# A fused layer on one core: one quarter of the expert values gathered by row instead of multiplied

## The chip, the core and the metric

The kernel runs on one core of a Trainium2 chip. The metric is device microseconds of that core; the time before is the median of three runs. The engines are named as the profile names them: PE (matmul), PEld (its weight load, which overlaps PE), DVE, ACT, POOL and SP. SP issues nearly all transfers, from one queue; 16 DMA engines carry them.

## The reference, cut to what matters

One layer with 256 tokens and 2048 channels. First a mixing block (projections, two kinds of linear attention, an output projection, LayerNorm). Then a product-key expert block, which is what the change touches:

```python
experts = ...   # per token 8 heads x 16 picks = 128 expert numbers i*128 + j
gates = softmax(top_s)                                     # per token 128 gates
act = gelu(einsum('tkd,td->tk', u_tab[experts], x))        # 128 activations a token
out = einsum('tk,tkd->td', gates * act, v_tab[experts])    # values, weighted and summed
h = layer_norm(alpha * h + out)
```

Both tables have 128 x 128 rows (experts) of 2048 channels in float32, 128 MB each.

## The kernel before, in words

Nothing is gathered. The kernel reads both tables whole and multiplies densely; the picks enter as a matrix of gates that is zero almost everywhere.

- **U stage, 128 tiles** (tile i holds the 128 experts with that i). SP loads 1 MB of `peer_u` in four pieces (`load_u`), DVE transposes it in quarters (`u_quarter`), ACT rounds it to the high part (`u_high`), POOL subtracts for the low part (`u_low`), PE multiplies (`u_tile`) into one of the PSUM banks 0, 1 and 7. ACT and DVE add the cross term, and ACT applies Gelu (`gelu`). For tiles 0 to 63 (near) the result goes into `act_w[:, 0]`; for tiles 64 to 127 (far) it stays in PSUM until DVE multiplies it into the gates (`weigh`).
- Between tiles 0 and 50 DVE works out the routing beside it (`route_*`): `ijg` gets i, j and gate of each pick. From tile 64 on DVE builds one-hot rows and columns of four tokens (`hot_rows`, `hot_cols`) and PE spreads the gates out by four small matmuls a tile (`spread`), which DVE multiplies into `act_w`. After this `act_w` holds gate times activation of every expert (partition j) for every token.
- **V stage, 128 tiles**, SP's loop over `load_v`: 1 MB of `peer_v` a tile, four slots; tile i is loaded when tile i-4 has been multiplied (`v_free`). ACT makes the high part of the tile's two halves and of the weights (`v_high`: `v_hi`, `m_hi`, `v_hi`), DVE the low parts (`v_low`: L1147 `v_lo`, L1149 `m_lo`, L1151 `v_lo`), and PE multiplies (L1604, `v_products`): high by high, high by low, low by high, for two blocks of 128 tokens (a), two halves of the channels (h) and two banks in each half (c), which is 3 x 2 x 2 x 2 = 24 matmuls of 512 columns a tile. All eight PSUM banks accumulate over all 128 tiles; bank 4a + 2h + c holds 512 channels of 128 tokens. `v_hi` has buffers for two tiles.
- In the V stage SP also loads `n_again`, `ln1g_sb` and `ln1b_sb` behind tile 67, from which POOL rebuilds the layer's input in eight blocks (L1268, L1270, from tile 70 on), and `ln2b_sb` and the last two value tiles (`v_late_raw`) behind tile 99. The last four value tiles are multiplied bank by bank, so that the final LayerNorm of a bank starts while PE is at the next.

The order on each engine is written out by hand; waits are on semaphores. DVE instructions that depend on the one before have a `drain` between them.

Of the kernel before, what the change touches and what calls it, by code (L numbers as in the profile page):

```python
# [25 lines left out]
F32 = mybir.dt.float32  # L26
# [24 lines left out]
U_PICK, U_TURN, U_SPREAD = 25, 51, 64  # L51
UR = 6
# [17 lines left out]
def constants():  # L70
    c = {}
    c["ident"] = np.eye(P, dtype=np.float32)
    c["iota"] = np.broadcast_to(np.arange(P, dtype=np.float32), (P, P))
    half = RDK // 2
    inv = np.float32(10000.0) ** (-np.arange(half, dtype=np.float32) / np.float32(half))
    ang = np.arange(T, dtype=np.float32)[None, :] * inv.astype(np.float32)[:, None]
    c["cos"], c["sin"] = np.cos(ang), np.sin(ang)
    t = np.arange(T)
    c["scan"] = np.broadcast_to((t % CH != 0).astype(np.float32), (P, T))

    m, n = np.meshgrid(np.arange(P), np.arange(P), indexing="ij")
# [7 lines left out]
    c["decay"] = np.concatenate([b for g in LOG_GAMMA for b in tiles(g)], axis=1)  # L89
    pack = lambda names: np.ascontiguousarray(np.concatenate([c[k].astype(np.float32) for k in names], axis=1))  # L90
    return pack(KEEP), pack(MIX)


def build(nc, x, w_in, w_up, b_gate, gla_g, ret_g, w_out, ln1_g, ln1_b, w_q, subkeys, peer_u, peer_v,
          ln2_g, ln2_b, keep_c, mix_c, out):
    ctx = ExitStack()
    with ctx:
# [67 lines left out]
        pick_ig = at("pick_ig", CST + 4608, [P, 2, T])  # L165
# [92 lines left out]
        v_hi_done, m_hi_done, v_lo_done, v_free, sum_done = sem("v_hi_done"), sem("m_hi_done"), sem("v_lo_done"), sem("v_free"), sem("sum_done")  # L258
        last_in, y_done, y_pool, out_done = sem("last_in"), sem("y_done"), sem("y_pool"), sem("out_done")
# [27 lines left out]
        def _(sp):  # L287
# [23 lines left out]
            with nc.allow_non_contiguous_dma(reason="512 bias values, one channel a partition"):  # L311
                sp.dma_start(bias4, b_gate[0].rearrange("(h p) -> p h", p=P)).then_inc(wup_in, 16)
            load(1, win, GQ + COL)
# [55 lines left out]
            with sp.Fori(U_TWO // 2, P // 2) as ii:  # L369
                for s in range(2):  # L370

                    sp.wait_ge(ut_done, ii * 8 + 4 * s - 4)
                    load_u(ii * 2 + s, s)

# [5 lines left out]
            for s in range(2):  # L380
                sp.wait_ge(ut_done, 4 * (P - 1) + 4 * s)
                load_v(s, s)
            sp.wait_ge(uparts_free, UR + 4 * P)
            for s in range(2, 4):
                load_v(s, s)

# [15 lines left out]
            for s in range(2):  # L402
                sp.dma_start(v_late_raw[:, 2 * s:2 * s + 2, :].rearrange("p a b -> p (a b)"), v_rows[P - 2 + s].rearrange("j d -> j d")).then_inc(v_late, 16)
            with sp.Fori(P // 4 - 7, P // 4 - 1) as ii:
                for s in range(4):
                    sp.wait_ge(v_free, ii * 8 + 2 * s + 2)
                    load_v(ii * 4 + s, s)
            for s in range(2):
                sp.wait_ge(v_free, (P // 4 - 1) * 8 + 2 * s + 2)
                load_v(P - 4 + s, s)  # L410
# [31 lines left out]
        def _(act):  # L442
# [42 lines left out]
            act.dma_start(keepc[:], keep_c).then_inc(keep_in, 16)  # L485
# [100 lines left out]
            def gelu(ii, j, far):  # L586

                act.wait_ge(u_sum, ii * 6 + j + 1)
                z = u_bank(j)[:, 0:T]
                act.activation(z if far else tile_w(0, ii * 6 + j), z if far else by_four(z), ACT.Gelu).then_inc(gelu_done, 1)  # L590
# [29 lines left out]
            for i in range(U_TURN // 6 * 6, U_SPREAD + 2):  # L620
                u_tile(i // 6, i % 6, 1)
                if i == U_TURN + 1:
                    act.wait_ge(ijg_mm, 1)
                    act.activation(pick_ig[:], ps[:, 4:6, 0:T], ACT.Copy).then_inc(ijg_sb, 1)
                elif U_TURN + 1 < i < U_TURN + 10:
                    ones(2 * (i - U_TURN - 2))
                    ones(2 * (i - U_TURN - 2) + 1)
            with act.Fori(U_SPREAD // 6 + 1, P // 6) as ii:
                for j in range(6):
                    u_tile(ii, j, 1, far=True)  # L630
# [89 lines left out]
        def _(dve):  # L720
# [345 lines left out]
            route_pick(1, 1, 2, 1)  # L1066
            with dve.Fori(U_TURN // 6, U_SPREAD // 6) as ii:
# [32 lines left out]
            def weigh(ii, j):  # L1100

                i = ii * 6 + j
                dve.drain()
                dve.wait_ge(gelu_done, i + 1)
                w = tile_w(1, i - P // 2)
                dve.tensor_tensor(w, w, by_four(u_bank(j)[:, 0:T]), ALU.mult).then_inc(gelu_free, 1)
# [21 lines left out]
            with dve.Fori(U_UNROLL // 6, P // 6) as ii:  # L1128
                for j in range(6):
                    u_spread_tile(ii, j)  # L1130
# [9 lines left out]
            def v_low(ii, s, half, last=False):  # L1140
# [6 lines left out]
                dve.tensor_tensor(lo_v[:, n, :], raw_v[:, n, :], vh[0].bitcast(F32), ALU.subtract)  # L1147
                dve.wait_ge(m_hi_done, ii * 4 + s + 1)
# [9 lines left out]
            with dve.Fori(1, P // 8) as ii:  # L1158
                for s in range(4):
                    v_low(ii, s, 0)  # L1160
            with dve.Fori(P // 8, P // 4 - 1) as ii:
# [7 lines left out]
            def last_bank(a, b):  # L1169

                c = slice(b * COL, (b + 1) * COL)
                dve.wait_ge(sum_done, 4 * a + b + 1)
                dve.scalar_tensor_tensor(h1_again[:, a, c], h1_again[:, a, c], float(ALPHA), bank(4 * a + b), ALU.mult, ALU.add).then_inc(bank_read, 1)
# [21 lines left out]
            dve.memset(power[:], -0.5)  # L1195
            for b in range(4):
                last_bank(0, b)
# [7 lines left out]
            last_bank(1, 3)  # L1205
# [6 lines left out]
        def _(pool):  # L1212
# [50 lines left out]
            pool.wait_ge(n_in, 48)  # L1263
            for a in range(TT):
                for b in range(4):
                    o, n_in_order = part(h1_again[:, a, :], 4 * b, 4), n_again[:, a, :].rearrange("p (f q l) -> p q f l", f=KT, q=4)[:, :, 4 * b:4 * b + 4, :]
                    pool.wait_ge(v_free, VRING + 2 * (P // 2 + 6 + 4 * a + b))
                    pool.tensor_tensor(o, n_in_order, part(ln1g_sb[:], 4 * b, 4), ALU.mult)  # L1268
                    pool.drain()
                    pool.tensor_tensor(o, o, part(ln1b_sb[:], 4 * b, 4), ALU.add).then_inc(h1_ready, 1)  # L1270
# [16 lines left out]
        def _(pe):  # L1287
# [308 lines left out]
            def v_products(s, h, a, start=False, last=False, stop=False, cs=range(2)):  # L1596
# [5 lines left out]
                for p, (m, v) in enumerate(((mh, vh), (mh, vl), (ml, vh))):  # L1602
                    for c in cs:
# [30 lines left out]
            for a in range(TT):  # L1634
                for b in range(4):
# [27 lines left out]
```

## Time and profile before

| | |
|---|---|
| time, median of 3 runs | 2042.71 us (2042.55 to 2043.31) |
| span of the profiled execution, first to last instruction | 2047.0 us |
| first and last start of a value matmul (L1604) | 1339.1 and 2035.5 us |
| PE busy | 2029.4 us, 99% |
| DVE busy | 1229.1 us, 60% |
| POOL busy | 1115.0 us, 54% |
| bytes moved | 381.35 MB |

No other time is given for the profiled execution than its span; it is 4.3 us (0.2%) above the median of the unprofiled runs. A busy time is the sum of an engine's instruction times. PE's instructions overlap, so its busy share tells only that it is never idle: the time of a matmul in a row of them is read from the chain, a stretch of time divided by the count.

### The profile page before, as it was taken

What the parts mean: (1) busy time and instruction counts of PE and PEld (TensorE: products, weight loads), DVE (VectorE), ACT (ScalarE), POOL (GpSimd) and SP (SyncE); (2) the same over time, 40 slices, a digit from 0 to 9 for tenths busy, and PEclk for the clock granted to TensorE, in tenths of its full rate; (3) what the DMA queues carried; (4) which work ended last, traced back from release to release, by engine and by line L of the source; (5) the groups of instructions that cost most, each with busy time, mean ns of one, the idle gap of its engine ahead of it and who ended that gap; (6) DMA issues with size and microseconds to landing.
All of it is one profiled execution on the core that took longest, in us unless ns stands there. A gap on an engine that the chain in (4) does not pass through costs nothing.

```text
span 2047.0 us, 34143 instructions
## 1 busy us (share of the span) xinstructions
PE 2029.4 (99%) x11214; PEld 1764.3 (86%) x11214; DVE 1229.1 (60%) x2134; ACT 980.1 (48%) x1454; POOL 1115.0 (54%) x720
## 2 busy tenths in 40 slices
PE   9999999999999999999999999999999999999997
PEld 8998888889988888888888888888888888888886
DVE  1753121122888777558998988955555556655556
ACT  4544334445455565674444444444444444444443
POOL 6877778877788989888777777700000002200001
PEclk9999999999999999999999999999999999999999
DMA  8555656577688887776666666665555557556552
GB/s 291 169 152 170 193 172 215 177 205 196 155 182 192 191 186 173 176 187 166 162 160 161 162 162 164 164 226 185 198 192 190 200 187 278 191 191 260 187 198 86
DMA packets 153540, 381.35 MB, mean 186 GB/s; under 512 B 19808, under 2 KB 22496, under 8 KB 135680
## 3 DMA queue, kind: packets, MB, share of 16 engines
q1 hardware_dynamic: 153328, 380.32, 64.9%
q8 instruction: 42, 0.69, 0.1%
q14 instruction: 26, 0.21, 0.0%
q10 hardware_dynamic: 144, 0.13, 0.0%
HBM read 376.20 MB, written 4.19 MB: 186 GB/s over the span
## 4 chain that ended last, share of the span: by engine, by line
PE 91%; POOL 3%; issue 3%; DVE 1%; DMA 1%; ACT 0%; DVEq 0%; POOLq 0%; ACTq 0%; SPq 0%
PE ps L1604 33%; PE ps L1563 22%; PE ps L1564 11%; PE ps L1303 7%; PE ps L1304 7%; PE ps L1305 7%; PE ps L1545 3%; POOL w_lo L1217 2%; POOL u_lo L1255 1%; PE ps L1419 1%; DMA raw<-in_w_in 0%; PE ps L1299 0%; PE ps L1528 0%; PE ps L1437 0%; DMA v_raw<-in_peer_v 0%
## 5 line engine op out<-in xcount | busy, mean ns | idle before, releaser
L1563 PE MATMUL ps<-xT,u_hi 128*128 128x512 f32 x2048 | 727.5, 399 | 0.5 <-POOL u_lo L1255 0.5
L1255 POOL TENSOR_TENSOR u_lo<-u_t,u_hi 128x512 fp32r<-128x512 f32 x512 | 653.1, 1298 | 129.4 <-ACT u_hi L579 127.2
L1564 PE MATMUL ps<-xT,u_lo 128*128 128x256 f32 x2048 | 573.3, 280 | 0.0
L579 ACT ACTIVATE u_hi<-u_t 128x512 fp32r<-128x512 f32 x512 | 321.2, 632 | 360.1 <-DVE u_t L961 359.5
L1217 POOL TENSOR_TENSOR w_lo<-raw,w_hi 128x1024 fp32r<-128x1024 f32 x174 | 424.1, 2449 | 107.5 <-ACT w_hi L448 101.2
L1563 PEld LDWEIGHTS ps<-xT,u_hi 128*128 128x128 f32 x2048 | 384.7, 188 | 90.7 <-issue 0.6
L961 DVE STREAM_TRANSPOSE u_t<-u_raw 128x512 f32<-128x512 f32 x512 | 356.0, 702 | 105.8 <-PE ps L1564 72.8
L1564 PEld LDWEIGHTS ps<-xT,u_lo 128*128 128x128 f32 x2048 | 386.6, 189 | 0.0
L1604 PE MATMUL ps<-v_hi,m_hi 128*128 128x512 f32 x1024 | 317.9, 389 | 0.0
L1604 PE MATMUL ps<-v_hi,m_lo 128*128 128x512 f32 x1024 | 317.8, 389 | 0.0
L448 ACT ACTIVATE w_hi<-raw 128x1024 fp32r<-128x1024 f32 x175 | 184.8, 1059 | 271.7 <-PE ps L1305 265.2
L1604 PE MATMUL ps<-v_lo,m_hi 128*128 128x512 f32 x1008 | 311.6, 389 | 0.0
L1268 POOL TENSOR_TENSOR h_again<-n_again,ln1g_sb 128x512 f32<-128x512 f32 x8 | 10.3, 1292 | 406.4 <-PE ps L1604 406.4
L1147 DVE TENSOR_TENSOR v_lo<-v_raw,v_hi 128x1024 fp32r<-128x1024 f32 x126 | 154.4, 1225 | 128.7 <-ACT v_hi L658 128.7
L1604 PEld LDWEIGHTS ps<-v_hi,m_hi 128*128 128x128 f32 x1024 | 192.1, 188 | 40.3 <-DVE m_lo L1149 0.5
L1604 PEld LDWEIGHTS ps<-v_hi,m_lo 128*128 128x128 f32 x1024 | 192.2, 188 | 40.0
L1604 PEld LDWEIGHTS ps<-v_lo,m_hi 128*128 128x128 f32 x1008 | 189.2, 188 | 39.3
L658 ACT ACTIVATE v_hi<-v_raw 128x1024 fp32r<-128x1024 f32 x124 | 131.6, 1061 | 159.2 <-PE ps L1604 146.6
L1151 DVE TENSOR_TENSOR v_lo<-v_raw,v_hi 128x1024 fp32r<-128x1024 f32 x126 | 163.0, 1293 | 45.2 <-ACT v_hi L663 45.2
L1303 PE MATMUL ps<-xT,w_hi 128*128 128x256 f32 x640 | 183.7, 287 | 3.5 <-DVE xT L716 3.1
L1305 PE MATMUL ps<-xT,w_lo 128*128 128x256 f32 x640 | 181.6, 284 | 0.0
L1304 PE MATMUL ps<-xT,w_hi 128*128 128x256 f32 x640 | 181.6, 284 | 0.0
(206 smaller groups left out, 2341.4 us busy)
## 6 DMA issues: line engine op xcount, KB each, us to landing
u_raw<-in_peer_u SPq DMA_DIRECT2D x512, 256.0 KB, 4.8
v_raw<-in_peer_v SPq DMA_DIRECT2D x126, 1024.0 KB, 4.9
raw<-in_w_in SPq DMA_DIRECT2D x111, 512.0 KB, 3.8
raw<-in_w_out SPq DMA_DIRECT2D x32, 512.0 KB, 4.8
raw<-in_w_peer_q SPq DMA_DIRECT2D x128, 128.0 KB, 3.4
x_again<-in_x SPq DMA_DIRECT2D x1, 2048.0 KB, 8.2
n_dram<-n_perm SPq DMA_DIRECT2D x1, 2048.0 KB, 8.1
n_again<-n_dram SPq DMA_DIRECT2D x1, 2048.0 KB, 9.3
```

The source lines that it names most:

```text
L448: act.activation(w_hi[:, k % HI_RING, :], raw[:, k, :], ACT.Copy).then_inc(hi_done, 1)
L579: act.activation(u_hi[:, slot(j, f), :], u_t[:, slot(j, f), :], ACT.Copy).then_inc(uhi_done, 1)
L961: dve.transpose(u_t[:, slot(j, f), :].rearrange("p (f b l) -> p b f l", f=4, b=4), u_raw[s][:].rearrange("p (b f l) -> p b f l", b=4, l=32 ...
L1151: dve.tensor_tensor(lo_v[:, n + 1, :], raw_v[:, n + 1, :], vh[1].bitcast(F32), ALU.subtract).then_inc(v_lo_done, 1)
L1217: pool.tensor_tensor(w_lo[:, k, :], raw[:, k, :], w_hi[:, k % HI_RING, :].bitcast(F32), ALU.subtract).then_inc(lo_done, 1)
L1255: pool.tensor_tensor(u_lo[:, r, :], u_t[:, r, :], u_hi[:, r, :].bitcast(F32), ALU.subtract).then_inc(ulo_done, 1)
L1303: pe.matmul(o, lh, rh, start=start, stop=False, skip_group_check=lint)
L1304: pe.matmul(o, lh, rl, start=False, stop=False, skip_group_check=lint)
L1305: return pe.matmul(o, ll, rh, start=False, stop=stop, skip_group_check=lint)
L1563: pe.matmul(acc, u_hi[:, r, c], xT[:, :, kt, :], start=kt == 0, stop=False)
L1564: ins = pe.matmul(acc[:, 0:T], u_lo[:, r, c], xT_hi[:, kt, :], start=False, stop=kt == KT - 1)
L1604: ins = pe.matmul(bank(4 * a + 2 * h + c), m, v[:, c * 512:(c + 1) * 512], start=start and p == 0, stop=stop and p == 2)
```

## The change

Bank 7 (tokens 128 to 255, channels 1536 to 2047) is no longer accumulated by PE. For each of these 128 tokens and each of its 128 picks, the quarter row of `peer_v` (512 channels, 2 KB) is gathered by POOL with an indirect DMA, one pick of all 128 tokens at a time, and DVE adds it, times gate and activation, into bank 7. For this:

- DVE works out two addresses a pick behind the routing (`place_picks`, tile 48). ACT writes them and the gates to DRAM.
- The activations are written to DRAM before the gates are multiplied in: the near ones in four transfers of 1 MB issued by ACT from tile 66 on, the far ones tile by tile by SP (64 KB each), for which ACT applies Gelu a second time to the upper 128 tokens (`far_act`). The Gelu of a far tile now goes into the other half of its bank.
- The gates for the one-hot columns are read from PSUM (bank 5) and no longer from SBUF.
- At the start of the V stage POOL loads addresses and gates, then issues 128 indirect DMAs that fetch one activation a token each (4 bytes x 128), then 128 that fetch rows, into eight slots. A row slot is refilled when DVE has added it. The eight blocks of L1268 and L1270 stand between the row groups 6 to 13.
- DVE waits for all activations at tile 44, multiplies them by the gates, and adds two rows in each of the tiles 44 to 107, between L1147 and L1149.
- PE's matmuls for (a, h) = (1, 1) take c = 0 alone: 21 a tile. In the last four tiles seven banks are left of eight.
- `v_late_raw` moves to where the row slots were, and its two transfers move behind the load of tile 123, after a wait for the last row. `h1_again` moves. Bank 7 is read first at the end, no longer last.

The diff, cut:

```diff
+            def far_store(n, s):
+                sp.wait_ge(far_done, n + 1)
+                sp.dma_start(act_far[bass.ds(n, 1)].rearrange("i j t -> (i j) t"), far_act[:, s, :]).then_inc(far_out[s], 16)
...
-            for s in range(2):
-                sp.dma_start(v_late_raw[:, 2 * s:2 * s + 2, :]..., v_rows[P - 2 + s]...).then_inc(v_late, 16)
             with sp.Fori(P // 4 - 7, P // 4 - 1) as ii:
                 for s in range(4):
                     sp.wait_ge(v_free, ii * 8 + 2 * s + 2)
                     load_v(ii * 4 + s, s)
+            sp.wait_ge(row_added, P)
+            for s in range(2):
+                sp.dma_start(v_late_raw[:, 2 * s:2 * s + 2, :]..., v_rows[P - 2 + s]...).then_inc(v_late, 16)
...
+                    act.activation(far_act[:, j % 2, :], z[:, P:T], ACT.Gelu).then_inc(far_done, 1)
+                act.activation(u_bank(j)[:, T:2 * T] if far else tile_w(0, ii * 6 + j), z if far else by_four(z), ACT.Gelu).then_inc(gelu_done, 1)
...
-                    ins = dve.tensor_scalar(hot_i[:, k, :], iota_ps, pick_ig[:, 0, t], pick_ig[:, 1, t], ALU.is_equal, ALU.mult)
+                    ins = dve.tensor_scalar(hot_i[:, k, :], iota_ps, pick_i[:, t], bank(5)[:, t], ALU.is_equal, ALU.mult)
...
+            def row_add(n, c):
+                dve.drain()
+                dve.wait_ge(row_in[c], n * 16 + 16)
+                dve.scalar_tensor_tensor(bank(7), sp_rows[:, c, :], sp_w[:, bass.ds(n * S_CHUNK + c, 1)], bank(7), ALU.mult, ALU.add).then_inc(row_added, 1)
...
+            dve.wait_ge(picks_in, 32)
+            dve.wait_ge(act_in, 16 * P)
+            dve.tensor_tensor(sp_w[:], sp_w[:], sp_gate[:], ALU.mult)
...
+            pool.wait_ge(uparts_free, UR + 4 * P)
+            for k in range(P):
+                pool.indirect_dma_start(sp_w[:, k:k + 1], None, act_dram, bass.IndirectOffsetOnAxis(ap=sp_at[:, 0, k:k + 1], axis=0)).then_inc(act_in, 16)
+            for n in range(S_END):
+                row_gather(n)
+                if n > 5 and n < 14:
+                    h1_block((n - 6) // 4, (n - 6) % 4)
...
-                    for c in cs:
+                    for c in cs if (a, h) != (1, 1) else (0,):
```

## Rows read from the trace of the kernel before

**Rows 1.** The page: span, then busy time and instructions of engines.
```profile
span 2047.0 us, 34143 instructions
PE 2029.4 (99%) x11214; PEld 1764.3 (86%) x11214; DVE 1229.1 (60%) x2134; ACT 980.1 (48%) x1454; POOL 1115.0 (54%) x720
```
**Rows 2.** The chain that ended last, in order of time: start, us, what.
```profile
1339.23 663.72 PE ps L1604 x2928
2002.97 4.99 DMA v_raw<-in_peer_v
...
2015.91 20.03 PE ps L1604 x87
```
**Rows 3.** Windows: busy us (instructions) of each engine, PEclk, DMA share, GB/s.
```profile
1180.00:1339.00 159.00, 159.00 (x983) 141.68 (x982) 142.24 (x291) 76.56 (x148) 121.52 (x95) 1.00 0.65 160
1360.00:1579.00 219.00, 219.00 (x968) 181.35 (x967) 115.69 (x121) 97.38 (x121) 0.00 (x0) 1.00 0.56 192
1690.00:1700.00 10.00, 10.00 (x46) 8.29 (x45) 4.88 (x7) 4.86 (x6) 0.00 (x0) 1.00 1.02 428
```
**Rows 4.** Waits from 1345 to 2000 us: us in total, times, longest.
```profile
ACT m_hi L661 <- PE ps L1604: 207.2, 118, 1.8
ACT v_hi L658 <- PE ps L1604: 145.4, 117, 1.4
DVE v_lo L1147 <- ACT v_hi L658: 126.9, 112, 5.0
...
ACT v_hi L658 <- DMA v_raw<-in_peer_v: 11.3, 4, 5.1
```
**Rows 5.** Timeline near the end: three DVE instructions with no wait between them.
```profile
2005.63 1.22 DVE L1147 TENSOR_TENSOR v_lo<-v_raw,v_hi 128x1024 fp32r<-128x1024 f32 x1
...
2006.77 0.42 DVE L1149 TENSOR_TENSOR m_lo<-act_w,m_hi 128x256 fp32r<-128x256 f32 x1
...
2007.10 1.22 DVE L1151 TENSOR_TENSOR v_lo<-v_raw,v_hi 128x1024 fp32r<-128x1024 f32 x1
```
**Rows 6.** Groups by form on DVE: count, busy us, mean ns, idle before.
```profile
L1090 DVE TENSOR_SCALAR hot_i<-ps,pick_ig 128x128 f32<-128x128 f32 x256 | 84.9, 394 | 0.0
...
L1098 DVE TENSOR_TENSOR act_w<-act_w,ps 128x512 f32 x54 | 37.1, 688 | 12.1 <-issue 12.1
...
L1173 DVE SCALAR_TENSOR_TENSOR h_again<-h_again,ps 128x512 f32<-128x512 f32 x8 | 5.5, 682 | 5.0 <-PE ps L1604 5.0
...
L704 DVE SCALAR_TENSOR_TENSOR h_again<-h_again,small,ps 128x512 f32<-128x512 f32 x5 | 3.7, 739 | 0.0
```
**Rows 7.** DMA issues on SP: count, KB each, median us from issue to landing.
```profile
u_raw<-in_peer_u SPq DMA_DIRECT2D x512, 256.0 KB, 4.8
v_raw<-in_peer_v SPq DMA_DIRECT2D x126, 1024.0 KB, 4.9
...
v_late_raw<-in_peer_v SPq DMA_DIRECT2D x2, 1024.0 KB, 10.3
...
ln1b_sb<-in_ln_b SPq DMA_DIRECT2D x1, 1024.0 KB, 13.3
```
**Rows 8.** POOL's groups, all forms: count, busy us, mean ns.
```profile
L1255 POOL TENSOR_TENSOR u_lo<-u_t,u_hi 128x512 fp32r<-128x512 f32 x512 | 653.1, 1298 | 129.4 <-ACT u_hi L579 127.2
...
L1217 POOL TENSOR_TENSOR w_lo<-raw,w_hi 128x1024 fp32r<-128x1024 f32 x174 | 424.1, 2449 | 107.5 <-ACT w_hi L448 101.2 <-DVE n_perm L927 6.2
```
**Rows 9.** Line L378, the issue of a value load: min/median/max ns.
```profile
L378 SPq DMA_DIRECT2D v_raw<-in_peer_v x126: 328/333/433, 1324.3 to 2003.0; - x126
```
**Rows 10.** Timeline where POOL's first block runs beside DVE.
```profile
1720.21 1.29 POOL L1268 TENSOR_TENSOR h_again<-n_again,ln1g_sb 128x512 f32<-128x512 f32 x1 [387.49 <-PE ps L1604]
...
1720.79 1.00 DVE L1149 TENSOR_TENSOR m_lo<-act_w,m_hi 128x256 fp32r<-128x256 f32 x1 [1.09 <-ACT m_hi L661]
1721.64 1.28 POOL L1270 TENSOR_TENSOR h_again<-h_again,ln1b_sb 128x512 f32<-128x512 f32 x1
1721.71 2.31 DVE L1151 TENSOR_TENSOR v_lo<-v_raw,v_hi 128x1024 fp32r<-128x1024 f32 x1
```

More of the change, by code:

```diff
@@ L51 @@
 U_PICK, U_TURN, U_SPREAD = 25, 51, 64
+FAR_COL = D - COL
+S_CHUNK, S_FIRST = 8, 11
+S_END = -(-P // S_CHUNK)
 UR = 6
@@ L385, in _ @@
                 load_v(s, s)
+            for s in range(2):
+                far_store(P // 2 - 2 + s, s)
             sp.wait_ge(spread_mm, P - U_SPREAD)
@@ L589, in gelu @@
                 z = u_bank(j)[:, 0:T]
-                act.activation(z if far else tile_w(0, ii * 6 + j), z if far else by_four(z), ACT.Gelu).then_inc(gelu_done, 1)
+                if far:
+                    if not isinstance(ii, int) or ii * 6 + j >= P // 2 + 2:
+                        act.wait_ge(far_out[j % 2], 16 * (ii * 3 + j // 2 - P // 4))
+                    act.activation(far_act[:, j % 2, :], z[:, P:T], ACT.Gelu).then_inc(far_done, 1)
+                act.activation(u_bank(j)[:, T:2 * T] if far else tile_w(0, ii * 6 + j), z if far else by_four(z), ACT.Gelu).then_inc(gelu_done, 1)
             def u_tile(ii, j, late=0, far=False):
@@ L623, in _ @@
                     act.wait_ge(ijg_mm, 1)
-                    act.activation(pick_ig[:], ps[:, 4:6, 0:T], ACT.Copy).then_inc(ijg_sb, 1)
+                    act.activation(pick_i[:], bank(4)[:, 0:T], ACT.Copy).then_inc(ijg_sb, 1)
+                    act.wait_ge(picks_done, 1)
+                    act.dma_start(at_dram, pick_at[:].rearrange("p s k -> p (s k)")).then_inc(picks_out, 16)
+                    act.dma_start(gate_dram, ijg[:, 2, 1, :]).then_inc(picks_out, 16)
                 elif U_TURN + 1 < i < U_TURN + 10:
+                    if i == U_TURN + 2:
+                        act.wait_ge(picks_out, 32)
                     ones(2 * (i - U_TURN - 2))
                     ones(2 * (i - U_TURN - 2) + 1)
-            with act.Fori(U_SPREAD // 6 + 1, P // 6) as ii:
+            for j in range(6):
+                u_tile(U_SPREAD // 6 + 1, j, 1, far=True)
+                if j < 4:
+                    if j == 0:
+                        act.wait_ge(gelu_done, P // 2)
+                    act.dma_start(act_near[:, 2 * K * j:2 * K * (j + 1)],
+                                  act_w[:, 0, P // 4 + 8 * j:P // 4 + 8 * (j + 1)].rearrange("p q i t -> p (q i t)")).then_inc(near_out, 16)
+            with act.Fori(U_SPREAD // 6 + 2, P // 6) as ii:
                 for j in range(6):
@@ L1066, in _, with place_picks @@
             route_pick(1, 1, 2, 1)
+            def place_picks():
+                i, j = ijg[:, 0, 1, :], ijg[:, 1, 1, :]
+                near, far, later, row = (pick_tmp[:, n, :] for n in range(4))
+                dve.wait_ge(tok_in, 16)
+                dve.drain()
+                dve.tensor_scalar(near, j, float(P * P // 2), tok[:, 1:2], ALU.mult, ALU.add)
+                dve.tensor_scalar(far, i, float(P * P), tok[:, 0:1], ALU.mult, ALU.add)
+                dve.tensor_scalar(later, i, float(P // 2), None, ALU.is_ge)
+                dve.tensor_scalar(row, j, float(D // COL), float(D // COL - 1), ALU.mult, ALU.add)
+                dve.drain()
+                dve.scalar_tensor_tensor(near, i, 4.0, near, ALU.mult, ALU.add)
+                dve.scalar_tensor_tensor(far, j, float(P), far, ALU.mult, ALU.add)
+                dve.scalar_tensor_tensor(pick_at[:, 1, :], i, float(P * D // COL), row, ALU.mult, ALU.add)
+                dve.drain()
+                dve.tensor_tensor(far, far, near, ALU.subtract)
+                dve.drain()
+                dve.tensor_tensor(far, far, later, ALU.mult)
+                dve.drain()
+                dve.tensor_tensor(pick_at[:, 0, :], far, near, ALU.add).then_inc(picks_done, 1)
+            place_picks()
             with dve.Fori(U_TURN // 6, U_SPREAD // 6) as ii:
@@ L1127, in _ @@
                 u_spread_tile(i // 6, i % 6, spreads=i > U_SPREAD + 1, weighs=i > U_SPREAD + 2)
-            with dve.Fori(U_UNROLL // 6, P // 6) as ii:
+            with dve.Fori(U_UNROLL // 6, 16) as ii:
+                for j in range(6):
+                    u_spread_tile(ii, j)
+            dve.wait_ge(near_out, 64)
+            with dve.Fori(16, P // 6) as ii:
                 for j in range(6):
@@ L1261, in _, with h1_block @@
                 u_low(P // 6, n)
[L1263 to L1270, printed above, removed]
+            def h1_block(a, b):
+                o, n_in_order = part(h1_again[:, a, :], 4 * b, 4), n_again[:, a, :].rearrange("p (f q l) -> p q f l", f=KT, q=4)[:, :, 4 * b:4 * b + 4, :]
+                pool.wait_ge(n_in, 48)
+                pool.wait_ge(v_free, VRING + 2 * (P // 2 + 6 + 4 * a + b))
+                pool.tensor_tensor(o, n_in_order, part(ln1g_sb[:], 4 * b, 4), ALU.mult)
+                pool.drain()
+                pool.tensor_tensor(o, o, part(ln1b_sb[:], 4 * b, 4), ALU.add).then_inc(h1_ready, 1)
@@ L1634, in _ @@
             for a in range(TT):
-                for b in range(4):
+                for b in range(4 - a):
                     for s in range(4):
```

89 lines of the change are left out of this document (74 added, 15 removed).

## The prediction

> **What bounds the kernel now.** I read the page first: PE is busy for 99% of the span [rows 1], so any gain must take work from PE. The chain that ended last gives the place: the value stage begins at 1339.2 us, and from there the chain is PE alone for 663.72 us and 2928 matmuls, and after a short passage through one transfer, ACT and DVE for another 20.03 us and 87 matmuls [rows 2]. That is 226.7 ns a matmul and, with 24 in a tile, 5.44 us a tile. The windows show that in this stage PE is never idle, at the full clock (2.4 GHz), DVE is busy 115.7 of 219 us, POOL not at all, and the DMA engines 0.56 of the time at 192 GB/s [rows 3]. The waits say who follows whom: ACT waits for PE to free the halves, DVE for ACT, and transfers are waited for 11.3 us in all [rows 4]. So in this stage PE is the bound and DVE, POOL and the transfers have room. In the last stretch of the U stage the picture is tighter: DVE 142 of 159 us, still with PE never idle [rows 3].
>
> **The change, part by part.**
>
> PE loses three matmuls in each of 128 tiles: 384 x 226.7 ns = -87.1 us [rows 2], if nothing else becomes the bound. A tile then takes 21 x 0.2267 = 4.76 us.
>
> DVE. Back to back, the three instructions of a tile start 1.14 and 0.33 us apart, and the third I count at 1.14 again: 2.61 us a tile [rows 5]. Before, that hides under 5.44. A row's addition is a scalar_tensor_tensor over 512 elements with one operand in PSUM and a scalar from SBUF; L704 is that form at 0.74 us, L1173 with a constant takes 0.68 [rows 6]. Writing to PSUM, not SBUF, I count at nothing. The drain in front costs what L1098 shows in a loop, 12.1 us over 54 = 0.22 us [rows 6]. A row is then 0.96 us, two of them 1.92, and a tile 2.61 + 1.92 = 4.53 us against PE's 4.76. So PE stays the bound in tiles 44 to 107 with 0.23 us to spare; I take 0 for this, and its bound above is 64 tiles times what DVE is over (0.3 us more a row would make 5.13 us a tile: +24 us). The U stage's DVE share of 0.89 without an idle PE [rows 3] says that an engine this full need not cost PE anything.
>
> POOL. No row shows an indirect DMA. The nearest prices are SP's issue of a load, 0.33 us [rows 9], below, and a POOL instruction over 1024 elements, 2.45 us [rows 8], above. I take the 512-element one, 1.30 us. The far activation of the last tile leaves ACT about 1 us into the V stage, its store stands behind two value loads (1 MB lands in 4.9 us [rows 7]) and the addresses are loaded after it, so the gathers start some 11 us in. 128 activation gathers end at 11 + 128 x 1.30 = 177 us, and DVE needs them at tile 44, at some 43 x 4.76 = 205 us. So there is no stall up to 1.5 us a gather. Row gathers need two a tile, 2.6 of 4.76 us, and eight slots are four tiles of lead, 19 us. I take 0; at 2.45 us the activations end at 325 us, 120 us late.
> The Trainium skill gives the price that no row here has: first byte of a transfer issued by POOL about 1 us ("DMA: Bandwidth & Descriptors", Latency and other measured facts), which as an estimate would end the activations 139 us into the stage, also hidden. The same page's fixed cost of about 2.0 us a transfer (Anatomy of one DMA) would, if POOL were held for all of it, end them at 267 us and stall DVE by some 60; the page calls it mostly completion, which POOL need not await.
>
> Transfers. A tile moves 1.05 MB, now in 4.76 us, plus 0.52 MB of rows: 330 GB/s in tiles 44 to 107. A window with a backlog shows 428 GB/s at share 1.02 [rows 3], so 330 fits, at about 0.8. The load of a tile is issued 4 tiles ahead, and ACT takes it up about 1.57 tiles later, 7.5 us against 4.9 to land. Behind tile 67 come 4 MB of other loads (the last of them landing after 13.3 us [rows 7]). Before, four waits of 11.3 us on ACT came out of it and the like, none on PE [rows 3, 4]. With shorter tiles and rows in between, 5 MB + 1.5 MB at about 400 GB/s land some 18 us after tile 63 is done, and PE needs them prepared by 19.0 - 4.3 = 14.8 us: +4 us, once.
>
> POOL's eight blocks. Beside one of them m_lo takes 1.00 and v_lo 2.31 us [rows 10] against 0.42 and 1.22 [rows 5]: 1.67 us more of DVE a block. Before, this lay in DVE's idle time. Now a block comes every fourth tile or so, and four tiles have 0.9 us of slack plus about 2 us by which DVE is ahead of PE. I count 0.75 us a block, +6 us.
>
> The U stage. `place_picks` is ten small instructions with drains, some 4 us of DVE once, under the ring of six quarters by which DVE is ahead. The one-hot columns now read a scalar from PSUM: each of four a tile takes 0.39 us [rows 6]; a scalar costs 0.06 (L704 against L1173), so up to that again, 0.24 us a tile, lies in DVE's 0.7 us of free time a tile. ACT's second Gelu is 128 elements beside 48% busy [rows 3]. The four near stores put 1 MB each beside a u tile of 1 MB that lands in 4.8 us; a tile here takes 6.6 us, so some lateness is taken up by the ring. SP's store waits for a Gelu that comes a tile before SP's next load is due. Together +3 us, between 0 and 64 x 0.2 = 13.
>
> The end. The late loads now stand behind tile 123: 3 MB are in the queue when tile 124 is loaded, and 2 MB took 10.3 us [rows 7]. Tile 125 lands as long after its issue as before (4.99 us [rows 2]) but two tiles of PE are now 1.4 us shorter: +1 us. DVE's last banks are reached with one application in front of bank 6: +1 us.
>
> Sum: -87.1 + 4 + 6 + 3 + 2 = -72 us on the span of 2047.0, which is 0.2% over the median; taken from the median, 2042.7 - 72 = 1971 us.
>
> **The rivals.**
>
> *DVE or the transfers become the bound of tiles 44 to 107.* For it: 0.23 us of slack is small, and the shares of the windows give another reading of the transfers: loads of the V stage at 192/0.56 = 343 GB/s, of the U stage, cut into shorter runs as the gathered rows are, at 160/0.65 = 246 [rows 3]; then a tile needs 3.06 + 2.13 = 5.19 us, +28 us. Against it: 428 GB/s in one window. With DVE 0.3 us over a row it is +24. Either gives about 1997, both together no more than 2010.
>
> *POOL is late.* At 2.0 us a gather the activations end at 267 us, +62: 2033. Beyond 2.08 us the change is slower than before, and at 2.45 it gives 1971 + 120 = 2091 us. For it: nothing but the missing row.
>
> *The gathers hold DVE off, the case on the other side.* 2.57 us of POOL work cost DVE 1.67 us in rows 10, 0.65 us for each. If address reading and issuing did the same, the 166 us of activation gathers would leave DVE 35% of its rate, 7.5 us a tile: 22 tiles in place of 35, +62 us; and two gathers a tile would add 1.69 to 4.53, 6.2 us a tile, 64 x 1.46 = +93. Together 1971 + 155 = 2126. It decides from 0.3 us lost for each us on, where it costs the 72.
> The Trainium skill says that a DVE instruction with two SBUF inputs contends with a POOL instruction that reads SBUF, one blocking the other wholly ("SBUF — State Buffer", Who interferes with whom); rows 10 agree (1.00 and 2.31 us). The page infers that descriptor generation needs only the write side, which `tensor_tensor` leaves free; taken so, this rival costs nothing, and taken as a POOL instruction like any other it costs the 155.
>
> *The change moves nothing*: not to be had, since the 384 matmuls are gone; it could only be hit by two costs that cancel.
>
> **How the numbers follow.** The forecast, PE the bound with small costs, 0.52; its own range 1956 (the 87.1 alone) to 1990. DVE or transfers the bound, 1990 to 2010: 0.18. POOL between 1.5 and 2.08 us a gather, or a mix of these, 2010 to 2038: 0.12. POOL beyond that or holding DVE off, above 2047: 0.16. The rest, 0.02, within 0.2% (4 us), which is about what a measurement of this kernel can tell from no change. Faster 0.82, same 0.02, slower 0.16. The range of 8 in 10 is 1956 to 2028: it leaves out the slower cases and the top of the third.
>
> **What would show it.** Right: 21 matmuls a tile at 227 ns in the value stage, PE never idle, a value stage of 610 to 625 us; POOL's gathers at 1.5 us or less; DVE at some 0.95 of the window in tiles 44 to 107, its rows at 0.74 us, v_lo still 1.22 us. Wrong: PE waiting for m_lo in every tile (DVE or rows late); a long wait of DVE at tile 44 for an activation; v_lo and m_lo longer throughout; ACT waiting for `v_raw`; PE idle in the U stage.

## The result and the profile after

The changed kernel takes 2022.9 us (median of 4 runs, 2014.9 to 2028.0) against 2043.0 (2042.6 to 2043.6): ratio 0.990, 95% interval 0.9873 to 0.9927. That is 20 us faster where 72 were forecast. The profiled execution, the slowest of the four, took 2028.0 us, with a span of 2026.2, 20.8 below that of [rows 1]. The page's first lines, and its two groups of indirect DMAs:

```profile
span 2026.2 us, 34413 instructions
PE 1962.4 (97%) x10830; PEld 1701.2 (84%) x10830; DVE 1311.5 (65%) x2274; ACT 989.1 (49%) x1518; POOL 1438.3 (71%) x978
...
L1392 POOL DMA_INDIRECT sp_rows<-in_peer_v,sp_at x128 | 160.1, 1251 | 76.7 <-DVE ps L1231 49.6
...
L1404 POOL DMA_INDIRECT sp_w<-act_dram,sp_at x128 | 158.7, 1240 | 48.3 <-issue 48.3
```

The 384 matmuls are gone, and PE now has idle time that [rows 1] did not have. The chain shows where (start, us, what; it answers to [rows 2]):

```profile
1339.24 209.68 PE ps L1742 x924
1548.92 14.23 issue
1563.16 8.06 PE ps L1742 x21
1571.29 7.73 another core or an unknown queue
1580.18 93.62 PE ps L1742 x399
1673.96 18.97 DMA v_raw<-in_peer_v
...
1697.72 21.52 PE ps L1742 x84
1719.25 8.14 issue
1727.38 15.24 PE ps L1742 x54
...
1870.56 107.80 PE ps L1742 x462
```

The stage starts at 1339.2 as before. Its first 44 tiles (924 matmuls) take 209.68 us: 226.9 ns a matmul, 4.77 us a tile. Then PE stops at 1548.9, 1575.5, 1687.9 and 1719.2 us, and for 3.6 us at 1867. Of the 21 matmuls at 1563.16 the first 14 start 439 ns apart, the rest 227 ns again: the granted clock is at half (1.2 GHz) until 1569.3. The waits from 1330 to 2020 us (in total, times, longest), beside [rows 4], name what was late:

```profile
ACT v_hi L718 <- DMA v_raw<-in_peer_v: 69.1, 32, 13.0
POOL sp_rows L1392 <- DVE ps L1231: 49.6, 39, 7.1
POOL sp_w L1404 <- issue: 48.3, 128, 6.1
...
POOL h_again L1382 <- issue: 43.4, 8, 8.4
...
PEld ps L1742 <- DVE m_lo L1244: 26.8, 12, 10.1
...
DVE ps L1231 <- DMA sp_rows<-in_peer_v,sp_at: 18.4, 9, 8.6
DVE sp_w L1259 <- DMA sp_w<-act_dram,sp_at: 16.1, 1, 16.1
POOL sp_at L1398 <- DMA act_dram<-far_act: 15.6, 1, 15.6
```

The windows (columns as in [rows 3]) show that the loss sits in a few places and is not a rate of every tile:

```profile
1360.00:1540.00 180.00, 180.00 (x796) 149.05 (x795) 108.89 (x113) 91.42 (x115) 142.62 (x112) 1.00 0.66 221
1540.00:1600.00 60.00, 41.43 (x157) 33.04 (x156) 30.06 (x37) 17.66 (x22) 36.40 (x35) 0.80 0.67 212
1600.00:1660.00 60.00, 60.00 (x266) 49.69 (x265) 51.43 (x63) 30.13 (x38) 33.67 (x26) 1.00 0.92 326
1660.00:1700.00 40.00, 30.34 (x129) 24.72 (x128) 25.86 (x31) 15.48 (x20) 13.43 (x11) 0.90 0.95 374
1700.00:1740.00 40.00, 31.86 (x124) 25.64 (x123) 24.88 (x30) 13.22 (x16) 19.35 (x16) 0.84 0.55 189
```

From 1600 to 1660, with two rows in every tile, PE is never idle and the clock is 1.00. From 1540 to 1600, 1660 to 1700 and 1700 to 1740 it is idle for 18.6, 9.7 and 8.1 us, and the granted clock is 0.80, 0.90 and 0.84: each of these pauses is followed by matmuls at 1.2 GHz.

The starts of L1742's matmuls give the ledger. The last one begins at 2013.1, so the stage takes 674 us where 128 tiles of 4.76 would be 609. Of the 65 us over it, tiles 43 to 46 have 25, tiles 67 and 68 have 12, tiles 71 and 72 have 11, tiles 88 to 100 have 8.5 (6.4 of it in tiles 99 and 100), the last four tiles 6.4 (two gaps of 2 us and the slow matmuls behind them), and the rest, 1.5, is small.

### The profile page after: what moved, and what is told of

The parts are those of the page before. It is cut to its first block, busy times and chain, and to the rows that moved or that the text cites. A ratio compares the mean times of both kernels' runs of the same rounds, so it can differ in the third digit from the quotient of the medians.

```text
span 2026.2 us, 34413 instructions
## 1 busy us (share of the span) xinstructions
PE 1962.4 (97%) x10830; PEld 1701.2 (84%) x10830; DVE 1311.5 (65%) x2274; ACT 989.1 (49%) x1518; POOL 1438.3 (71%) x978
## 4 chain that ended last, share of the span: by engine, by line
PE 78%; issue 7%; POOL 6%; DMA 3%; DVE 3%; DVEq 1%; ACT 1%; another core or an unknown queue 0%; POOLq 0%; SPq 0%; ACTq 0%
PE ps L1742 23%; PE ps L1701 20%; PE ps L1702 10%; PE ps L1441 7%; PE ps L1443 7%; PE ps L1442 7%; PE ps L1683 3%; POOL w_lo L1329 2%; POOL u_lo L1367 2%; DMA v_raw<-in_peer_v 1%; DMA sp_rows<-in_peer_v,sp_at 1%; DVEq L1229 1%; DVE v_lo L1240 1%; DMA u_raw<-in_peer_u 1%; DVE ps L1231 1%
## 5 line engine op out<-in xcount | busy, mean ns | idle before, releaser
L1742 PE MATMUL ps<-v_hi,m_hi 128*128 128x512 f32 x896 | 297.2, 400 | 44.7 <-issue 22.4
L1742 PE MATMUL ps<-v_hi,m_lo 128*128 128x512 f32 x896 | 293.3, 395 | 0.0
L1742 PE MATMUL ps<-v_lo,m_hi 128*128 128x512 f32 x882 | 287.9, 395 | 0.0
L1742 PEld LDWEIGHTS ps<-v_hi,m_hi 128*128 128x128 f32 x896 | 171.2, 193 | 85.9 <-DVE m_lo L1244 26.8
L1240 DVE TENSOR_TENSOR v_lo<-v_raw,v_hi 128x1024 fp32r<-128x1024 f32 x126 | 157.1, 1247 | 90.3 <-ACT v_hi L718 86.2
L1392 POOL DMA_INDIRECT sp_rows<-in_peer_v,sp_at x128 | 160.1, 1251 | 76.7 <-DVE ps L1231 49.6
L1742 PEld LDWEIGHTS ps<-v_hi,m_lo 128*128 128x128 f32 x896 | 171.7, 192 | 36.6
L1742 PEld LDWEIGHTS ps<-v_lo,m_hi 128*128 128x128 f32 x882 | 169.2, 192 | 36.1
L1404 POOL DMA_INDIRECT sp_w<-act_dram,sp_at x128 | 158.7, 1240 | 48.3 <-issue 48.3
```

The costliest lines, as they stand in the source:

```text
L1742: ins = pe.matmul(bank(4 * a + 2 * h + c), m, v[:, c * 512:(c + 1) * 512], start=start and p == 0, stop=stop and p == 2)
```

## The experiments

All times are medians, all ratios to the kernel before as run on the same chip. The unchanged kernel's own median there was 2042.8, 2044.0 and 2045.2 us in the three sittings.

**Rows begin one step later (e1_first12).** DVE takes up the rows at tile 48, not 44.
```
-S_CHUNK, S_FIRST = 8, 11
+S_CHUNK, S_FIRST = 8, 12
```


> The first row addition is moved from tile 44 to tile 48, nothing else. Theory A (the wait for the last activation at tile 44, and PE's lower clock behind it, cost the 25 us by which tiles 43 to 46 are longer than 4.76 us): the activations end at 1558 us, tile 48 is reached by DVE at about 1561, so the stall goes and the time falls by 20 to 25 us, to about 2000. Rival B (tiles with additions are as slow as DVE, POOL or the transfers make them, and the stall only comes out of that): the time stays within 8 us of the changed kernel, at 2015 to 2028. In both the long tiles 67, 68, 71 and 72 stay, or the last two get shorter, since the row groups come four tiles later beside POOL's blocks.

1993.3 us, ratio 0.9755 [0.9737, 0.9773]: 30 us less than the change as it stands. The wait of DVE for an activation is 2.7 us in place of 16.1, and in the stretch that had 18.6 us of idle PE and a clock of 0.80:
```profile
1540.00:1600.00 60.00, 58.86 (x259) 48.05 (x258) 44.36 (x54) 29.57 (x37) 42.80 (x35) 1.00 0.86 308
```
The 30 us are more than the 20 to 25 expected, because the move did two things. By tile, in the profiled executions, tiles 43 to 46 lose their excess of 25 us (1.5 comes back in tiles 47 and 50). Tiles 71 and 72 lose theirs of 11 as well, now that the rows come four tiles later beside POOL's blocks, and tiles 67 and 68 grow by 2. The late activations, about 24 us, are still the largest single loss.

**POOL's blocks behind all row gathers (e2_blocks_last).**
```
 for n in range(S_END):
     row_gather(n)
-    if n > 5 and n < 14:
-        h1_block((n - 6) // 4, (n - 6) % 4)
+for n in range(8):
+    h1_block(n // 4, n % 4)
```


> POOL's eight blocks (two instructions with a drain between) stand behind the last row gather, no longer between the row groups. Theory A (the drain of POOL waits 5.4 us on the mean for gathers still under way, 43.4 us in all, and the rows behind it come late): the gaps before the second instruction of a block go, the tiles 71, 72, 88, 89, 96, 99 and 100 lose their excess of 20 us together, and the time falls by 12 to 20 us. Rival B (those tiles are long because DVE's low parts are held by POOL's two instructions, as in the kernel before): the gaps go too, but the additions still take their time and the time falls by less than 6 us. The stall at tile 44 stays in both.

2013.4 us, 0.9847 [0.9831, 0.9864]: -9.5, between the two expectations (12 to 20, under 6) and not much beside the 13 us over which the change's own four runs spread. The pause at tile 71 is gone, the one behind tile 67 stays, and some of the gain goes back in tiles 106 to 108 (7.3, 6.5 and 5.3 us), where the eight blocks now run back to back beside DVE. Of their drains only the first, right behind the last gathers, leaves a gap: 5.8 us, against 0.14 in the other seven.

**The same, with the 4 MB of other loads spread (e3_blocks_last_loads_spread).** Eight pieces of 0.5 MB, one behind every third tile's load from tile 69 on.
```
+for i in range(P // 2 + 4, P - 28):
+    sp.wait_ge(v_free, 2 * i + 2)
+    load_v(i, i % 4)
+    if i % 3 == 0 and once:
+        sp.dma_start(*once.pop(0)).then_inc(n_in, 16)
```


> As the kernel with the blocks last, and the 4 MB that SP loads behind tile 67 (layer input, gain, bias) are cut into eight pieces of 0.5 MB, one behind every third tile from 69 on. Theory A (this burst keeps the value loads behind it waiting, 12 us in tiles 67 and 68): another 10 to 12 us less than with the blocks last alone, and ACT's longest wait for a value load falls from 13.0 to under 4 us. Rival B (the transfers are at their limit throughout the tiles with rows, so the 4 MB cost the same wherever they stand): less than 4 us, the waits are spread over more tiles.

1997.2 us, 0.9784 [0.9760, 0.9808]: -16 against e2. The same stretch in e2 and then here:
```profile
1660.00:1700.00 40.00, 29.07 (x129) 23.78 (x128) 24.34 (x31) 15.48 (x20) 15.30 (x13) 0.90 0.97 378
```
```profile
1660.00:1700.00 40.00, 39.42 (x174) 32.32 (x174) 33.30 (x41) 19.64 (x26) 21.25 (x17) 1.00 0.96 346
```
The DMA engines were at 0.97 and 0.96. What PE gained is 174 matmuls for 129, because the value loads no longer stand behind a burst: from 1640 to 1700 ACT's longest wait for `v_raw` is 13.8 us in e2 and 3.4 here.

**All three together (e5_all_moved).** Besides, the two late loads are issued inside the last tile loads.
```
+if i in (P - 12, P - 9):
+    s = (i - P + 12) // 3
+    sp.wait_ge(row_added, P)
+    sp.dma_start(v_late_raw[:, 2 * s:2 * s + 2, :]..., v_rows[P - 2 + s]...)
```


> All moved: first addition at tile 48, blocks last, the 4 MB spread, and the two loads of the last value tiles put behind the loads of tiles 116 and 119 in place of behind tile 123. Theory A (four separate waits, none of them a rate): PE without a pause and at its full clock from tile 0 to 123, 4.76 us a tile, the time at 2042.7 - 87 + 6 = 1962 us, between 1957 and 1972. Rival B (a rate of DVE, POOL or the transfers of about 5 us in tiles with rows): 16 us more, 1975 to 1990.

1976.4 us, 0.9663 [0.9644, 0.9682]: 4 us above the 1957 to 1972 of theory A and inside the 1975 to 1990 of rival B, so the time alone speaks for B. The windows speak against it. Two windows, in the stage's middle and where the blocks now run:
```profile
1580.00:1700.00 120.00, 119.98 (x529) 99.00 (x529) 104.56 (x127) 60.67 (x76) 66.58 (x50) 1.00 0.94 341
```
```profile
1840.00:1880.00 40.00, 35.06 (x152) 27.80 (x151) 35.58 (x35) 18.38 (x23) 25.71 (x18) 1.00 0.73 247
```
With rows in each tile and 341 GB/s, PE is idle for 0.02 of 120 us: neither DVE's 4.5 us a tile (the forecast's sum) nor the transfers are a bound. What is left is 8 us in tiles 107 to 112 (109 and 110 take 7.3 each), where the blocks run back to back, 3.8 in tiles 99 and 100, where SP loads `ln2b_sb` whole, and 4.2 in tiles 47 and 48.

**No gathers and no additions (f1_no_gather).** This leaves the gathered rows out of the result, and the waits on them with it.
```
-for k in range(P):
-    pool.indirect_dma_start(sp_w[:, k:k + 1], ...)
 for n in range(S_END):
-    row_gather(n)
```


> The changed kernel without its 256 gathers and 128 additions (and the waits on them): bank 7 of the values is left out of the output. All stores of the U stage stay. Theory A (the 384 matmuls are worth 87 us, and the U stage's additions cost nothing): 2042.7 - 87 + 2 to 5 = 1958 to 1961 us, ACT and DVE with less work than before. The burst behind tile 67 costs a few us at most, since no rows compete with it. Rival B (the 21-matmul tile is itself limited by ACT, DVE or loads): over 1970 us.

1966.7 us, 0.9619 [0.9603, 0.9635]. The stage's last matmul starts at 1953.7, 614.7 us after its first. So 77 of the 87 us are there once the gathers and additions are gone. The time lies between the two expectations (1958 to 1961, over 1970). Of the missing 10 us, 5 are in the stage, which is 614.7 us where 128 tiles would be 609: 1.4 in tile 67 (the burst) and 3.6 in the last four tiles (the late loads), both still in place here. One more is behind the last matmul, 12.4 us against 11.4; the rest this run does not place.

**A semaphore in place of the drain in a block (s1_sem_for_drain).**
```
-pool.tensor_tensor(o, n_in_order, part(ln1g_sb[:], 4 * b, 4), ALU.mult)
-pool.drain()
+pool.tensor_tensor(o, n_in_order, part(ln1g_sb[:], 4 * b, 4), ALU.mult).then_inc(h1_half, 1)
+pool.wait_ge(h1_half, 4 * a + b + 1)
```


> The changed kernel with the drain between POOL's two instructions of a block replaced by a semaphore that the first one raises and the second waits for; the blocks stay between the row groups. Theory A (the drain waits for gathers that POOL has issued and that are still in work; the first instruction itself is done after 1.3 us): the gap before the second instruction falls from 5.4 us to under 0.3 us, rows are no longer late behind a block, and the time falls by 8 to 15 us. Rival B (the first instruction's writes, or POOL itself, are held up for those 5 us by something else, such as DVE's reads): the gap stays at about 5 us and so does the time.

2014.5 us, 0.9856 [0.9839, 0.9872]: -8.5; its four runs (2012.7 to 2015.7) just overlap the change's (2014.9 to 2028.0), so the rows say more than the time. The first block on POOL's timeline after the change, with the gathers behind it, and then here:
```profile
1709.88 1.32 POOL L1380 TENSOR_TENSOR h_again<-n_again,ln1g_sb 128x512 f32<-128x512 f32 x1 [26.52 <-PE ps L1742]
1717.18 1.29 POOL L1382 TENSOR_TENSOR h_again<-h_again,ln1b_sb 128x512 f32<-128x512 f32 x1 [5.97 <-issue]
1718.61 0.98 POOL L1392 DMA_INDIRECT sp_rows<-in_peer_v,sp_at  x1
```
```profile
1707.83 1.32 POOL L1381 TENSOR_TENSOR h_again<-n_again,ln1g_sb 128x512 f32<-128x512 f32 x1 [25.78 <-PE ps L1743]
1709.23 1.29 POOL L1383 TENSOR_TENSOR h_again<-h_again,ln1b_sb 128x512 f32<-128x512 f32 x1
1710.66 0.99 POOL L1393 DMA_INDIRECT sp_rows<-in_peer_v,sp_at  x1
```
The 6 us between the halves of a block were the drain, waiting for gathers in flight, as the single long one of e2 says too; over eight blocks 43.4 us, here 0.6. Tile 71 falls from 13.1 to 8.3 us, yet PE still pauses for 3.8 while gathers go out unbroken. That asked for the next group.

**The low part of the values by a one-input instruction (g3_one_input).** The low part is then the value itself and the result differs; the instruction's price on DVE is that of the two-input form (1.22 us in both).
```
-dve.tensor_tensor(lo_v[:, n, :], raw_v[:, n, :], vh[0].bitcast(F32), ALU.subtract)
+dve.tensor_reduce(lo_v[:, n, :], raw_v[:, n, :].unsqueeze(2), AX.X, ALU.add)
```


> The changed kernel with DVE's two v_lo instructions of a tile made from one SBUF input in place of two (a reduction over one element, as many elements out; the low part is then the value itself, so the output differs). Theory A (a gather is held from 0.94 to about 1.95 us where DVE is in an instruction with two SBUF inputs; its long ones end as v_lo does): the gathers of activations take 0.94 to 1.1 us each, 1.25 to 1.35 from start to start, the last ends 160 to 175 us after the first in place of 201, and DVE does not wait at tile 44. Rival B (the long gathers come from the loads that share the transfer engines, or from the gather's own bookkeeping): a mean of 1.24 us and 201 us as before, DVE's wait of 16 us stays.

2157.6 us (2 runs), 1.0554 [1.0533, 1.0575]: 135 us slower than the change, which neither theory had. The gathers did get shorter, but this alone does not clear the two-input form, since DVE hardly ran beside them (15 instructions in the window below):
```profile
L1406 POOL DMA_INDIRECT sp_w<-act_dram,sp_at x128 | 121.3, 947 | 47.6 <-issue 47.6
```
But while they go out, PE hardly does (window, then PE's timeline):
```profile
1360.00:1545.00 185.00, 44.75 (x125) 29.16 (x124) 13.18 (x15) 10.95 (x14) 126.25 (x134) 0.57 0.14 40
```
```profile
1417.40 0.59 PE L1744 MATMUL ps<-v_lo,m_hi 128*128 128x512 f32 x1 [2.21 <-issue]
1420.20 0.59 PE L1744 MATMUL ps<-v_hi,m_lo 128*128 128x512 f32 x1 [2.21 <-issue]
```
PE waits for nothing here that the profile shows; its matmuls come 2.8 us apart. So it goes in the second half of tiles 7, 8 and 9, with one matmul in 0.7 to 3.5 us, and in front of each of these tiles PE stands still for 26 to 31 us. So two explanations were tried next: the new DVE form, or the unbroken train of gathers.

**One input without gathers (r1_one_input_no_gather), and one input with paced gathers (p1_one_input_paced).** The pace holds activation gather k until PE has passed tile k/3.
```
+    pool.wait_ge(v_free, VRING + 2 * (k // 3 + 1))
     pool.indirect_dma_start(sp_w[:, k:k + 1], None, act_dram, ...)
```


> The kernel with one-input low parts and no gathers and no additions at all (bank 7 and the low parts differ). Theory A (the gathers slow PE, not the DVE form): 4.76 us a tile throughout and within 3 us of the kernel without gathers, 1966.7 us. Rival B (the DVE form does): long tiles 6 to 9 again and over 2080 us.

> The kernel with one-input low parts (its output differs) and the activation gathers paced: gather k waits until PE has multiplied tile k/3, so about three a tile, 1.59 us apart on the mean in place of 1.25. Theory A (an unbroken train of gathers 1.25 us apart slows the other engines' sequencers, which is why PE's matmuls stood 2.8 us apart in tiles 6 to 9 of the kernel with one-input low parts): tiles 6 to 9 take 4.76 us each, and the time falls from 2157 by at least 120 us. A short slow patch at the first tiles is possible, where the pace lets twelve through at once. Rival B (the other form of DVE instruction slows PE, or the loads): tiles 6 to 9 stay long, about 2150 us.

1966.8 us, 0.9616 [0.9593, 0.9640], and 2012.7 us, 0.9841 [0.9820, 0.9862]. The window of g3 in r1, then in p1:
```profile
1360.00:1545.00 185.00, 185.00 (x818) 153.19 (x817) 111.22 (x117) 94.47 (x117) 0.00 (x0) 1.00 0.64 221
```
```profile
1360.00:1545.00 185.00, 180.83 (x781) 147.80 (x780) 105.60 (x111) 88.68 (x111) 109.91 (x118) 0.98 0.63 211
```
The DVE form does not slow PE. A pace on the same gathers gives back 145 us, and what is left of the slow stretch are tiles 6 and 7 (11.1 and 6.8 us), where the gathers let through by the first waits go out unbroken. What it is in the unbroken train that stops the other engines, no run shows.

**The kernel before once more (p0_before_again)**, unchanged, one profiled run.

> The kernel before, once more, for a second profile. Its first profile has a span of 2047.0 us, 4 us over the median time, while every changed kernel's span is 1.8 us under the time of the same execution. Theory A (that first profiled execution was a slow one by some 6 us, ahead of the value stage): this span is about 2041 us and the value stage begins at 1333 us, so that the changed kernels, which begin it at 1336 to 1339, carry 3 to 6 us from the U stage. Rival B (the first profile was an ordinary one): 2047 us and 1339 us again, and the U stage costs nothing.

2046.2 us, span 2044.4, value stage from 1336.7 to 2033.0: between the two expectations. The start of the stage moves by 2 to 4 us from run to run in both kernels (1336.7 and 1339.1 before, 1335.9 to 1340.3 in the changed ones), so the U stage's part of the change costs nothing that shows beyond that.

**The best of these (b1_spaced), and with the pace (b2_spaced_paced).** e5, with one block a tile from tile 111 on and ln2b loaded in four pieces.
```
-pool.wait_ge(v_free, VRING + 2 * (P // 2 + 6 + 4 * a + b))
+pool.wait_ge(v_free, VRING + 2 * (P - 16 + 4 * a + b))
```


> The kernel with everything moved, and two more steps: POOL's eight blocks wait for tiles 111 to 118, one a tile, and the load of the last bias (1 MB behind tile 99) is cut into four pieces. Theory A (back to back, the blocks hold DVE to a third of its rate over tiles 107 to 112, 9 us in all, and the 1 MB behind tile 99 costs the 4 us of tiles 99 and 100): both excesses go, 10 to 13 us less than with everything moved, 1963 to 1967 us. Rival B (tiles 99 and 107 to 112 are long because the value loads are late from transfers at 0.95 of their capacity all along): 1972 to 1978 us, with ACT's waits for loads of some 97 us unchanged and the long tiles elsewhere.

> The kernel with everything moved and spaced (1967.4 us), and the activation gathers paced by PE's tiles as well (k/3). Theory A (what is left at tile 47, 1.6 us, is the end of an unbroken train): tile 47 back at 4.76 us, the time lower by 1 to 3 us, hardly to be told from none. Rival B (pacing lets the gathers end later than the additions need them): tile 47 longer than 6.4 us and a time over 1969 us.

1967.4 us, 0.9625 [0.9602, 0.9647], and 1965.8 us, 0.9610 [0.9594, 0.9626]: 77 and 79 us under the kernel before in the same sitting and some 56 under the change, as fast as the kernel that gathers nothing. In f1 the late loads and the burst were still in place, so this equality does not make the gathers free: b1's stage is 615.3 us, 6 more than 128 tiles of 4.76. With every gather and every addition in it, b2's middle looks so:
```profile
1560.00:1860.00 300.00, 295.22 (x1298) 242.97 (x1298) 256.13 (x311) 147.56 (x185) 164.89 (x127) 1.00 0.95 344
```
The pace makes no difference that can be measured here (the intervals overlap). Tile 47, which theory A had back at 4.76 us, stays at 6.4, and tile 49 takes 7.8. That the two-input form breaks the train by itself, so that a pace has nothing to add, is our reading.

## Why the prediction was right and wrong

The forecast was 1971 us, with a range of its own from 1956 to 1990; 2022.9 lies outside that, and inside the wide range of 8 in 10 (1956 to 2028). It also lies in the band of 2010 to 2038 that the forecast gave to gathers of 1.5 to 2.08 us or a mixture, at 0.12. The price did come out in there, at 1.57. But by the forecast's own sum this price would have added 7 us and not 52, so that the band was hit by several terms together. Two of its signs of being wrong were seen, the long wait of DVE at tile 44 and ACT waiting for `v_raw`.

**Right: the 87.1 us.** 21 matmuls a tile at 227 ns, and PE never idle where nothing is late (1360 to 1540, 1600 to 1660). f1 keeps 77 of it, b2 79.

**Right: DVE stays under PE, and the transfers fit.** A row's addition takes 0.756 us and a wait of 0.2 in front, 0.96 in all, as forecast; tiles stay at 4.76. DVE's share from 1600 to 1660 is 0.86 and not 0.95, since the two waits of 0.2 us a tile don't count as busy. The forecast 330 GB/s were 326 to 344, though at a share of 0.92 to 0.95, not 0.8. The DVE-or-transfers rival is out: at 5.19 us a tile 120 us would hold 485 matmuls, and e5 has 529.

**Right: the gathers do not hold DVE off.** While the activation gathers go out, L1240's v_lo takes 1225 to 1227 ns, L1246's 1211 to 1248 and m_lo 424 to 427, against 1.22 and 0.42 in [rows 5], so the slower case (2126 us) is out. The longer ones (v_lo up to 2.32 us) come later, beside POOL's blocks. It is the other way round. The timeline of all engines:
```profile
1380.25 0.94 POOL L1404 DMA_INDIRECT sp_w<-act_dram,sp_at  x1 [0.30 <-issue]
...
1381.41 1.23 DVE L1240 TENSOR_TENSOR v_lo<-v_raw,v_hi 128x1024 fp32r<-128x1024 f32 x1 [1.09 <-ACT v_hi L718]
...
1381.50 1.95 POOL L1404 DMA_INDIRECT sp_w<-act_dram,sp_at  x1 [0.30 <-issue]
...
1383.76 0.94 POOL L1404 DMA_INDIRECT sp_w<-act_dram,sp_at  x1 [0.31 <-issue]
1383.86 1.22 DVE L1246 TENSOR_TENSOR v_lo<-v_raw,v_hi 128x1024 fp32r<-128x1024 f32 x1 [0.41 <-ACT v_hi L723]
```
A gather takes 0.94 us, also when v_lo begins behind it, but 1.95 when it starts early in a v_lo that is running. Of the 128 activation gathers 39 start with more than 0.15 us of a v_lo left, and 37 of these take over 1.2 us; no other one takes over 1.03. A row gather that starts inside a row addition (39 do) is not held either: 0.94 to 0.98. That it takes the two-input form of v_lo shows from p1 beside b2, with the same pace: 16 gathers of p1 start in this way in the one-input v_lo and take 0.94 to 1.03, 44 of b2 in the two-input one and take 1.12 to 1.97, 1.96 in the middle. The Trainium skill ("SBUF — State Buffer", Who interferes with whom) infers that descriptor generation is left free by `tensor_tensor`. By that, DVE is indeed not delayed, but POOL is, so the inference holds for one side only.

**Wrong: "POOL, 0 us" (1.30 us a gather from 11 us in, done at 177).** The step that failed is the price taken for a gather and the date of the first. The price was good for one gather (1.25 from start to start), but the mean over the train, with three in ten held by DVE, was 1.57: 200 us from the first start to the last where 166 were forecast. And the first gather starts at 1355.8, 16.6 us in and not 11, since the address load waits for the far store (15.6 us) and then has to land. The last starts at 1555.8, which is 217 us in, against 205 needed. The forecast had named no stall up to 1.5 us a gather, and 1.57 went past it. DVE waits 16.1 us, once:
```profile
1558.28 0.36 DVE L1259 TENSOR_TENSOR sp_w<-sp_w,sp_gate 128x128 f32<-128x128 f32 x1 [16.11 <-DMA sp_w<-act_dram,sp_at]
```
With the pauses and the low clock behind it this costs 25 us (tiles 43 to 46); e1 gets back about 24 of it, and 30 in all.

**Wrong: "POOL's eight blocks, +6".** The forecast priced the block's two instructions beside DVE and left out its drain. Behind a gather the drain waits 5.4 us a block, rows come late, and the eight gathers held back go out unbroken. Ledger 19.5 us (tiles 71, 72 and 88 to 100); moved (e2) or undrained (s1) the times are 9.5 and 8.5 lower. Not all of the 19.5 is the blocks': SP loads `ln2b_sb` behind tile 99, and where the blocks stand behind the gathers but this load is whole (e5), tiles 99 and 100 still have 3.8 of their 6.4 us. With the load in four pieces (b1) they have none.

**Mis-sized: "the burst behind tile 67, +4".** The mechanism was right: ACT waits for `v_raw` at tile 67, up to 13.0 us. The term measured 12 in the ledger and 16 between e2 and e3; without rows (f1) it is 1.4.

**Right to within a few us: the U stage (+3, measured 0).** **Mis-sized: the end (+2).** The last four tiles are 6.4 us over, and 13.1 us lie behind the last matmul in place of 11.4: 8 in all. Tile 125 was to land as long after its issue as before; the chain has 7.15 us for a load there, in place of 4.99, behind the two late loads. Where these are issued earlier (e5), the last four tiles are 1.4 over.

**Missed altogether: what a pause costs afterwards.** Behind each of the five stops of 3.6 us or more, and behind the two of 2 us in the last tiles, 11 to 14 matmuls start some 440 ns apart and not 227. The granted clock is at 1.2 GHz for 7 to 17 us each time, part of it while PE still stands. PE's gaps are 46 us, and the slow matmuls add 18: 64 of the 65 us over.

The sum by what was measured: -87 + 25 (activations) + 12 (burst) + 19.5 (blocks and `ln2b_sb`) + 6.5 (last four tiles) + 1.5 (small) = -22.5 for the stage; 1.7 us more behind it gives the -20.8 of the span.

**Still open.** Why PE stops a second time at 1575.5 for 4.7 us after the activations have come; what keeps tile 47 at 6.4 us in b1 and b2, and tile 49 at 7.8 in b2; why the changed kernel's times spread over 13 us and the kernel before's over 1 to 6 in the four sets of runs; and which resource the unbroken train takes. That the train is also what stops PE at 1718.9 is argued from g3 and p1 and from the eight gathers 1.25 us apart there (PE restarts when the last is out), but no run changed that train alone.

## What to carry to other kernels

A change that takes work from the bound of a stage is worth its price only if every producer's pieces come in time: the losses here were a few waits, none of them a rate, and moving their dates, with no less work, was worth some 56 us. Give work that runs once (a train of gathers, a burst of loads, blocks on POOL) slack or an even pace, and never put a drain behind gathers in flight, where a semaphore on the one instruction will do. When a price has two rows, alone and beside another engine's access, take the mean that the stage will really have, and count a stall of PE with the slow clock behind it.

## What the runs showed of the hardware

- An indirect DMA of 128 elements or 128 rows of 2 KB holds POOL for 0.94 us, and the next starts 0.30 us later. If it starts while a two-input DVE instruction over 1024 elements runs it takes up to 1.98 us, in a one-input one of the same length (p1) 0.94 to 1.03, and DVE's instruction is as long as ever (1.22 us).
- While 128 gathers went out 1.28 us apart without a break (g3, 162 us), PE, ACT and DVE all but stood: 125 matmuls in 185 us in place of 818, at a DMA share of only 0.14, and the kernel took 2157.6 us; with a wait in front of each gather, 2012.7.
- A POOL drain behind gathers waited 5.4 us on average, one with no gather before it 0.14 (e2), the semaphore on the instruction itself 0.1 (s1).
- PE idle for 3.6 to 15 us came back at 1.2 GHz: 11 to 14 matmuls some 440 ns apart in place of 227, for 5 to 6 us (in e1 a stop of 3.7 us was not followed by them). In g3's slow window the mean granted clock was 0.57.
